# Moving the input scaling of the experts into their own phase, and reordering the work around three phase borders

## The reference

```python
# mixer: two branches, each gated by a sigmoid, then the output product and the residual
y = sigmoid(m_hg) * y_hg + sigmoid(m_gla) * y_gla
x = x + mod[2] * (y @ w_o)
# experts: norm, scale and shift, then 8 query heads and 16384 experts
h = modulate(rmsnorm(x, norm_ffn_g), mod[3], mod[4])
q = h @ wq                        # 16 tiles of 128 columns
# scores against two sets of 128 keys, top 16 x top 16, softmax of the best 16: gates g_e
# out = sum_e g_e * gelu(u_e . h) * v_e
x = x + mod[5] * out
x = rmsnorm(x, final_g)
# second block, four times:
x = layer_norm(ALPHA * x + (1.0 + gate) * y, g, b)
```

## Time and profile before

| | us |
|---|---|
| median of 3 runs | 3967.69 |
| lowest, highest | 3964.88, 3970.22 |
| the profiled execution | 3967.14 |
| its span | 3965.2 |
| PE busy | 3749.0 (95%) |
| DVE busy | 2275.7 (57%) |
| ACT busy | 1645.4 (41%) |
| POOL busy | 1104.5 (28%) |

### The profile page before, as it was taken

The page is one execution under the profiler, slowest core; times in us unless marked ns, Lnnn a source line. Parts: engine busy times, 40 slices in busy tenths (PEclk is TensorE's granted clock), DMA queues, the critical chain, the costliest instruction groups (busy, mean ns, idle before and its releaser), DMA issues. The chain is left out here.

```text
span 3965.2 us, 47057 instructions
## 1 busy us (share of the span) xinstructions
PE 3749.0 (95%) x18178; PEld 3110.0 (78%) x18178; DVE 2275.7 (57%) x3599; ACT 1645.4 (41%) x2239; POOL 1104.5 (28%) x646
## 2 busy tenths in 40 slices
PE   7999799989799999999999999998999998789998
PEld 6888677768688888888878888886778887677886
DVE  6555445344366666755457777776555465855353
ACT  5555454444322234544444444445543223434222
POOL 1222122144244443333344444442020003502002
PEclk9999999899899999999999999999999999999999
DMA  4111011055134444355588888882023332132331
GB/s 177 56 51 54 24 59 43 11 191 196 59 126 126 132 130 187 114 197 204 197 269 268 263 265 268 267 266 72 32 75 97 103 97 63 34 95 74 101 96 64
DMA packets 226410, 515.87 MB, mean 130 GB/s; under 512 B 23792, under 2 KB 98800, under 8 KB 224016
## 3 DMA queue, kind: packets, MB, share of 16 engines
q1 hardware_dynamic: 203968, 408.89, 32.3%
q0 software_dynamic: 18720, 68.17, 5.3%
q10 hardware_dynamic: 3504, 35.85, 2.2%
HBM read 438.64 MB, written 69.21 MB: 128 GB/s over the span
## 5 line engine op out<-in xcount | busy, mean ns | idle before, releaser
L1349 PE MATMUL peer_banks<-peer_h_parts,peer_w_parts 128*128 128x512 f32 x3456 | 801.1, 392 | 13.9 <-POOL peer_w_parts L1542 13.9
L1349 PEld LDWEIGHTS peer_banks<-peer_h_parts,peer_w_parts 128*128 128x128 f32 x3456 | 646.9, 188 | 146.9 <-POOL peer_w_parts L1542 14.1
L1349 PE MATMUL peer_banks<-peer_act_parts,peer_w_parts 128*128 128x512 f32 x3072 | 697.9, 390 | 9.4 <-DVE peer_act_parts L1838 9.4
L1349 PEld LDWEIGHTS peer_banks<-peer_act_parts,peer_w_parts 128*128 128x128 f32 x3072 | 577.7, 188 | 129.6 <-issue 9.8
L1542 POOL TENSOR_TENSOR peer_w_parts<-slots,peer_w_parts 128x1024 fp32r<-128x1024 f32 x144 | 344.5, 2393 | 570.7 <-ACT peer_w_parts L1670 570.7
L1349 PE MATMUL ffn_ps<-h_parts,ffn_w_parts 128*128 128x512 f32 x1920 | 450.2, 396 | 19.6 <-DVE h_parts L2445 10.9
L1670 ACT ACTIVATE peer_w_parts<-slots 128x1024 fp32r<-128x1024 f32 x272 | 286.9, 1055 | 390.9 <-PE peer_banks L1349 389.5
L1349 PEld LDWEIGHTS ffn_ps<-h_parts,ffn_w_parts 128*128 128x128 f32 x1920 | 364.9, 190 | 103.6 <-DVE ffn_w_parts L2289 15.6
L1349 PE MATMUL ffn_ps<-ffn_hidden,ffn_w_parts 128*128 128x512 f32 x1920 | 439.8, 391 | 2.3 <-DVE ffn_hidden L2352 2.3
L1349 PEld LDWEIGHTS ffn_ps<-ffn_hidden,ffn_w_parts 128*128 128x128 f32 x1920 | 361.5, 188 | 79.1 <-issue 3.9
L175 POOL TENSOR_TENSOR peer_slab<-peer_slab 128x1024 f32<-128x1024 f32 x96 | 236.7, 2466 | 335.2 <-ACT peer_slab L182 334.8
(11 more groups left out here) (546 smaller groups left out, 5419.3 us busy)
## 6 DMA issues: line engine op xcount, KB each, us to landing
slots<-in_peer_u SPq DMA_DIRECT2D x128, 512.0 KB, 3.6
slots<-in_peer_v SPq DMA_DIRECT2D x128, 512.0 KB, 4.8
slots<-in_mlp_w SPq DMA_DIRECT2D x128, 512.0 KB, 3.5
peer_slab<-in_w_mod POOLq DMA_DIRECT2D x96, 512.0 KB, 4.2
peer_acts<-h SPq DMA_DIRECT2D x128, 256.0 KB, 2.4
peer_gates<-peer_slab ACTq DMA_DIRECT2D x16, 2048.0 KB, 16.6
peer_slab<-peer_acts SPq DMA_DIRECT2D x128, 256.0 KB, 5.1
peer_slab<-peer_gates SPq DMA_DIRECT2D x128, 256.0 KB, 5.5
```

Source lines behind the costliest of these rows:

```text
L1349: last = nc.tensor.matmul(out, w(a, k), x(b, k), start=start and k == ks[0] and n == 0, stop=stop and k == ks[-1] and n == 2)
```

## The change

Seven edits:

1. The experts' scaled input is made in `peer` instead of `mix_out`. `mix_out` ends with the root of the mean square, kept in `K.h[:, 0, :]`; `normed`, `parts_high` and `parts_low` now stand at the head of `peer`, with tile 0 taken last. DVE, not POOL, makes the low parts of the first two weight tiles.
2. The two query tiles of head 0 run interleaved, input tile by input tile (`first_queries`).
3. In `mix_out` the 32 sums of `mod` stand otherwise: one per tile in both `SIG` stretches, two per tile in the first `BRANCH` stretch, none in the second.
4. In the second `BRANCH` stretch DVE takes `gate_second`, `merged_low`, and the low part of the weight tile last.
5. `load_pair(0)` and `(1)` are issued two weight tiles ahead of the end of `u`; `act_high(0)` and `(1)` stand ahead of the last gelu; DVE weighs first and splits `v` tile 1 last.
6. At the end of `peer` POOL adds the first six squares in pairs, and PE multiplies five tiles by ones instead of eight.
7. A one-column `Ln` is put ahead of the last squares (in `mix_out`, `peer`, and both norms of `ffn`), so that the table is loaded there.

```diff
-                    M.sum(act, n)
+                    M.sum(act, 3 * KT * half + k)
...
-                    M.sum(act, n)
+                    if half == 0:
+                        M.sum(act, KT + 2 * k)
+                        M.sum(act, KT + 2 * k + 1)
...
+            A(tiny[:], K.ones[:, 0:1], ACT.Ln)
             square(KT - 1)
             act.wait_ge(sum_done, 1)
-            st.then(A(rstd[:], s2[:], ACT.Ln, scale=1.0 / D, bias=EPS))
-            A(rstd[:], rstd[:], ACT.Exp, scale=-0.5).then_inc(root, 1)
...
+            st.then(A(K.h[:, 0, :], s2[:], ACT.Ln, scale=1.0 / D, bias=EPS))
+            st.then(A(K.h[:, 0, :], K.h[:, 0, :], ACT.Exp, scale=-0.5))
...
             store(U_TILES - 1)
-            for n in range(4):
-                load_pair(n)
+            load_pair(2)
+            load_pair(3)
...
-            for p in range(FRONT):
+            for p in range(2, FRONT):
                 g.wait_ge(w_hi, p + 1)
...
+            for k in (0, 2, 4):
+                g.wait_ge(sq_done, k + 2)
+                nc.gpsimd.tensor_tensor(K.h[:, k, :], K.h[:, k, :], K.h[:, k + 1, :], ALU.add).then_inc(paired, 1)
...
+            def first_queries():
+
+                pe.wait_ge(w_lo, 2)
+                for i, k in enumerate(ORDER):
+                    pe.wait_ge(h_lo, i + 1)
+                    for s in range(2):
+                        last = parts_product(nc, q_ps[:, s * T:(s + 1) * T], weights(s), lambda a, k: hp[:, a, k, :], (k,), i == 0, i == KT - 1)
+                        if i == KT - 1:
+                            last.then_inc(used, 1)
...
             high(0)
+            parts_high(0)
             high(1)
+            for i in range(1, KT):
+                parts_high(i)
...
+                    if n == U_TILES - 1:
+                        act_high(0)
+                        act_high(1)
...
+            normed(0)
+            normed(1)
+            first_low(0)
+            normed(2)
+            parts_low(0)
+            first_low(1)
+            for i in range(1, KT):
+                if i + 2 < KT:
+                    normed(i + 2)
+                parts_low(i)
```

More of the change, by code:

```diff
@@ L1748, in _ @@
                 act.wait_ge(s, 16 * TT)
+            A(iota[:, 0:1], K.ones[:, 0:1], ACT.Ln)
             for k in range(KT):
```

103 lines of the change are left out of this document (57 added, 46 removed).

## The result

The changed kernel takes 3946.3 us (median of 5 runs, 3945.6 to 3948.8); the kernel before, run beside it, 3970.0 (3964.9 to 3972.8). The ratio is 0.9943, with a 95% interval of 0.9933 to 0.9954: 0.6% faster. The forecast was 3944.5, within 3936 to 3954. The profiled execution took 3945.7 us, its span 3943.8 (3965.2 before). PE is busy for 3745.4 us (3749.0 before), so 17.8 of the 21.4 us by which the span is shorter came out of PE's idle time, and 3.6 us out of its busy time.

A forecast was written before the change was run, and what follows sets the result against it. PE, busy 95% of the span, bounds the kernel, so gains come only where it waits or runs at its lower clock. 3.9 + 3.6 + 10.7 + 2.6 + 1.8 = 22.6 us off 3967.1 gives 3944.5 us, range 3936 to 3954.

The forecast's parts named there:

- The long wait: In mix_out, PE's 7.58 us wait for the low part of the third `WO` tile, forecast to go.
- the two tiles named: First `BRANCH` stretch of mix_out: PE waits 1.9 us for tile 18 and 2.2 us for tile 19, 4.1 us lost.
- The pair of rounds: First `BRANCH` stretch of mix_out: two rounds of sum and multiply per tile take 7.67 us against PE's 5.44.
- 7P - 49.6: PE's stall in mix_out's first `BRANCH` stretch, in us, for a pair of rounds of length P.
- the 9.6 us: Gain in mix_out's second `BRANCH` stretch: the 7.58 us wait ahead of `WO` and 2.05 us of low clock.
- The border: From mix_out's sum of squares to peer's third query tile: 3.6 us won, between 1.5 and 7.5.
- The 2.0 us charged for the clock: Loss to a fall of PE's clock at the new 3.6 us wait ahead of peer's third tile.
- reserve for pair 2: From `u` to `v`: the gain is 9.7 us instead of 10.7 if pair 2 lands a microsecond late.
- The end of peer: Sum of squares in peer: five products by ones instead of eight win 2.6 us, 1.3 at the lower end.
- The norms: Four layer norms: the early table load wins 1.8 us, between 0 and 2.0, capped by DVE's own two subtractions.
- the rivals: Late pairs at `v` 3950.5 us (0.08), longer rounds in mix_out 3950.3 (0.13), border without gain 3948 (0.08), slower kernel (0.02).
- the rival of a slower kernel: Doubled sums in mix_out with a pair of rounds over 12.1 us; 3977 us at 12.5; chance 0.02.

The follow-up runs named there:

- experiment 9: Changed kernel with the 32 sums of `mod` placed as in the kernel before, one per tile; DVE's new order in the second `BRANCH` stretch kept: 3941.5 us.
- experiment 10: Changed kernel with DVE's order in the second `BRANCH` stretch as before the change; the sums of `mod` stay as the change has them: 3945.4 us.
- experiment 8: Changed kernel with the 24 sums of `mod` of mix_out's first half spread evenly, alternately one and two per tile: 3945.9 us.
- experiment 3: Changed kernel with the first two query tiles of peer one after the other instead of interleaved: 3942.3 us.
- experiment 7: Changed kernel with the first two query tiles interleaved for five input tiles, then the last three of tile 0, then those of tile 1: 3943.4 us.
- experiment 5: Changed kernel with eight products by ones, no pairs on POOL, plus one tiny POOL addition waiting for the end of peer's sum of squares: 3949.3 us, one run.
- experiment 6: Changed kernel with DVE instead of POOL subtracting the last means, so DVE does all eight tiles in the four layer norms: 3932.6 us.

## Why the prediction was right, point by point

**mix_out: mechanism right, 3.1 us too little.** The long wait went as told, and the new waits stood at the two tiles named. Two terms were too large. The waits themselves: 2.1 us by the profile, 2.8 by the length of the stage (experiment 9), for 4.1. The pair of rounds took 7.46 us and not 7.67; put into the forecast's own 7P - 49.6 that gives 2.6. The step that failed is the longer of the two rounds, 3.95 us, taken from another stretch. There DVE splits a tile of `y` as the multiply begins, and both that multiply (2.62) and the low part (2.87) are longer:

```profile
836.85 0.68 DVE L1265 TENSOR_TENSOR y_parts<-h,y_parts 128x512 fp32r<-128x512 f32 x1
```

At the two late tiles no such split stands before the multiply, POOL keeps its 2.39 us, and DVE's low part alone is stretched (2.64). And the fall of the clock (1.6) did not come: 1.00 throughout. What the forecast missed altogether is that the doubled sums were not needed (experiments 9 and 10): it had given the 9.6 us to the two edits together, and they are had by either one (9.7 us in experiment 9, from the ninth tile to the sum of squares).

**The border: each time right within 0.3 us, the clock wrong.** Start of peer 9.3 us after the sum of squares (9.5), first matmul 4.85 (5.0), both query tiles 18.2 (18.0), the new wait 3.38 (3.6). The 2.0 us charged for the clock did not come. Experiments 8 and 9 show that it can come: behind a wait of the same length it came twice in ten traces. That it did not come here was luck as far as the forecast goes, since nothing in it could tell the two cases apart. By these ten traces the price is 0 to 2.7 us, 0.4 in the mean. The third tile started 5.8 us earlier, against 5.6 without the charge. One more us or so was to be had: run one after the other, or with the last input tiles of tile 0 first, the two query tiles bring the third one 1.3 us sooner (experiments 3 and 7).

**`u` to `v`: right, 9.9 of 10.7 us.** The wait went whole (9.45 us). The forecast's own reserve for pair 2 ("If it is a microsecond late, 9.7") came true in another way: the pair was there in time, but its weighing stood beside POOL's multiply.

**The end of peer: 1.9 of 2.6, and 2.4 lost behind it.** Without the early table it would have been 2.5 (9.10 us against 11.64 with eight products), which is the forecast. The step that failed is "in peer the load was already under PE's products: nothing": it was right for the load where it was, and wrong for where it went, ahead of the squares that feed the pairs. POOL's three adds took 3.80 us, 1.27 each, so DVE's residuals beside them did not stretch them, as the forecast had it. The border was not in the forecast at all. It asked who waits for the moved adds, but asked it of PE alone, and not of the barrier behind them, which POOL's last instruction holds up longest (experiment 5).

**The norms: 0 of 1.8.** The forecast capped the gain by DVE's own subtractions and did not look at POOL's, 6.8 us beside them in the trace of before. The Trainium skill ("SBUF — State Buffer", two separate sides) has a DVE instruction with two SBUF inputs and a GpSimd one that reads SBUF exclude each other; the trace agrees, with 3.25 us for two scalings that take 1.29 when POOL is still (experiment 6). The forecast had used this very rule in mix_out and not here.

So the total came out 1.8 us off by the medians, and 1.2 by the profiled executions (21.4 us for 22.6), while single terms were off by up to 3.1 in both directions: mix_out and the border gave 5.3 more, the other stages took 7.4 away, and 0.9 came from a part that nobody touched. That the total is so much nearer than its terms is luck. None of the rivals happened. Two slips of arithmetic changed little: (2708.04 - 2701.01)/8 is 0.88 and not 0.86, and for a pair of rounds of 12.5 us the rival of a slower kernel comes to 3978 and not 3977.

## What to carry to other kernels

When two edits are aimed at one wait, undo each alone before paying for both: here the cheaper one, an order of three instructions, would have done all of the work. Before an engine is given work at the end of a phase, look at what its last instruction releases, and before a shorter step is counted, look at what the other engines run beside it until the next one begins (here POOL's subtractions beside DVE's scalings). A wait that goes from 2.3 to 0.9 us can pay twice, once in itself and once in the clock behind it.

## What was not expected of the hardware

- The granted clock after a short wait of PE: it stayed at 1.00 behind waits of 0.87, 1.36, 1.68 and 2.03 us, fell behind 2.28 and 2.31 us in the norms, and behind 3.38 us fell in two traces of ten. The length of the wait alone does not decide it: in the changed kernel it also fell behind 2.02 us, ahead of the second norm, while behind the 2.03 us of experiment 7 it stayed. What decides it is not shown, but the place in the program counts: ahead of the first norm's weight tile (2.24 to 2.33 us) it fell in all twelve traces that have this wait.

```profile
3273.80 1.12 PE L2077 MATMUL ffn_sum<-ffn_rest,ones 128*128 128x512 f32 x2 [2.02 <-POOL ffn_rest L2142]
```

```profile
3274.90:3278.30 3.40, 3.31 (x5) 1.51 (x5) 0.00 (x0) 0.00 (x0) 0.06 (x1) 0.51 0.00 0
```

- 9.77 us from the end of POOL's last instruction to its first one behind the border with the clearing of the semaphores, the same in all traces where POOL had worked late (with two and with three pairs, and with a single column); with POOL idle for longer, ACT stood there 1.94 us.
- 28 spare matmuls at the end of mix_out gave nothing back: with 8 of them the 48 matmuls of the first queries took 13.36 us, with 28 of them 13.34.
